# A two-layer decoder step: the last expert pair added by a one-hot product, the first pair's tokens picked by one-hot products, a separate place for the mixing weights

## The chip, the core and the metric

One core of one Trainium2 chip runs the whole step. The metric is device time in microseconds (us) of one execution, the median of several runs; lower is better.

## What is computed

Two layers over 288 tokens (256 of a prompt, 32 of eight decoding sequences), model width 1024, all in float32. Layer 0 mixes tokens by latent attention, layer 1 by a spatial gating unit. After the mixer each layer adds a mixture of experts and then a gated projection ("ple"):

```
pg = softmax(t @ w_rg + b_rg)              # 4 groups, top 1
pe = softmax(le of that group)             # 8 experts, top 2
w  = pg_top * pe_top / sum(pe_top)
y  = sum over the 2 experts of w * (silu(t @ w_gate) * (t @ w_up)) @ w_down
h  = h + y
h  = h + sigmoid(rmsnorm(h) @ w_ple_gate) * (p @ w_ple_proj)
```

with 32 experts of hidden width 256. So a token belongs to exactly two experts, both of one group, and they may or may not be in the same pair of experts.

## The kernel before, in words

**Weights.** All weights lie in HBM as a stream of 250 slots of 1 MB. SyncE loads them in order into a ring of 12 slots (`load_slot`, `load_rounds`); a load waits for the semaphore `slot_free`, which TensorE raises as it uses up slots. The slots of one layer's experts are six per pair: four with gate and up weights, two with down weights. Before them stands one slot with the projection of `ple`, behind them four with its gate. The third gate slot and all behind it wait for `y12_in2`, the landing of the last `y12` load.

**Routing** (`moe(L)` on each engine). TensorE forms the router's sums. VectorE (L848 to L887) finds group and experts, computes the rank of each token in its expert, and from that a row number `row`: two experts form a pair, each with a window of 64 rows, 128 rows in all. ScalarE takes one exponential (L563) for the routing weights, in the middle of copying the eight tiles of the projection `prj` out of PSUM (L565; TensorE makes them in `project`, L1325). `members(n)` (L895, L899) builds for pair n the one-hot table `member` (six blocks of 128x128: first and second expert choice, by three token tiles) and steps `row` on. `list_pair` (L1334) multiplies it with token numbers and weights, and `take_list` (L903, L904) stores the token number and destination row of the 128 rows in `slots`, and the weights in `gr`.

**Pairs.** For each of the 16 pairs GpSimd gathers the tokens' rows from HBM (`gather`, L335) into `x_sel`, two buffers. TensorE transposes them (`x_turn`, L1360), ScalarE and VectorE copy the halves into `xT` (L569, L917), TensorE runs gate and up (L1374), ScalarE and VectorE form the activation (L573, L922), TensorE transposes it (L1367), ScalarE copies (L577), TensorE runs down (L1383), and the result, scaled by the routing weight, goes into `y_sb` (L581 ScalarE, L927 VectorE). GpSimd scatters it to `y_rows` in HBM (`scatter`, L344): 2 x 288 rows, one for each token and choice. If an expert has more than 64 tokens, a loop on all engines (`If(most > WIN)`) does the rest in further passes; with these inputs it is skipped.

**Combination and gate.** When the scatter of the last pair has landed, GpSimd loads `y_rows` into `y12` with six transfers (L400). VectorE adds the two choices (L976), TensorE transposes 128-column tiles of the sum (`combine`, L1457), VectorE adds them to `h` (L688) and multiplies by the gain (L692). TensorE then runs the first tile of the gate (`gate_part`, L1446), mixed with the transposes and with eight products that sum the squares for the norm (`square_part`, L1462; ScalarE squares, L609). ScalarE takes the root (L457), VectorE the reciprocal (L708); then follow seven more tiles of eight products. In layer 0 ScalarE, after the root, starts three loads: the spatial mixing weights `ws` and `wss` and their bias `bs` (L613). Their place in memory overlaps `y12`. VectorE masks them (L984, L985), and TensorE sums their columns (L1486, L1488) behind the third gate tile.

**End.** After the last norm VectorE scales the even tiles of the output, GpSimd the odd ones (L422); ScalarE issues all eight stores, even ones first (L643, L646).

The lines that say most of this are:

```
pool.wait_ge(sem(f"y_put{L}_{b}"), 16 * (PAIRS // 2))       # before the y12 loads, both b
pe.wait_ge(sem(f"x_got{L}_0"), 16)                           # before the first x_turn
pe.wait_ge(sem("comb"), 3 * L + 3)                           # before the first combine
pe.wait_ge(sem("ws_m"), 2)                                   # before L1486
```

## Time and profile before

| | |
|---|---|
| median of 3 runs | 1240.37 us (1238.86 to 1242.16) |
| the profiled execution | 1241.1 us, span of its instructions 1239.3 us |
| TensorE busy | 1081.3 us, 87% of the span |
| VectorE, ScalarE, GpSimd busy | 363.0, 193.5, 112.8 us |
| transfers | 306.80 MB, mean 248 GB/s |
| mean granted TensorE clock | 0.94 of 2.4 GHz |

How the views are read. A line of the *timeline* has the start, the busy time, the engine (PE TensorE's products, PEld its weight loads, DVE VectorE, ACT ScalarE, POOL GpSimd, SP SyncE; with a q, its queue issuing a transfer), the line of the kernel, the operation, output<-inputs and their shapes, how many instructions are merged, and in brackets the idle time before and what ended it. TensorE needs two passes for a float32 product, so the profile shows two instructions for each, while a transpose is one. A line of a table of *windows* has the window, its length, the busy time (and instructions) of PE, PEld, DVE, ACT and POOL, then the granted clock (1.00 is 2.4 GHz, 0.50 is 1.2 GHz), the busy share of the 16 transfer engines, and GB/s. The *chain of waits* follows the work that ended last back to the start and gives shares of the span.

### The profile page before, as it was taken

The numbers are of one execution on the slowest core, as the hardware profiler recorded it, in microseconds if no ns is written. First come the engines' busy times: TensorE is split into PE (matmuls) and PEld (weight loads), VectorE is DVE, ScalarE is ACT, GpSimd is POOL, SyncE is SP. The second block draws the span as 40 slices with busy tenths as digits, with TensorE's granted clock in tenths as the row PEclk, the third lists the DMA queues.
The fourth block names the chain that finished last, engine by engine and source line by source line (L and its number), as shares of the span: only waits on it lengthen the run. The fifth ranks groups of instructions, "written<-read, shape, count | busy, mean of one in ns | idle before, by whom it ended". The sixth has DMA issues, their size and how long they took to land.

```text
span 1239.3 us, 14327 instructions
## 1 busy us (share of the span) xinstructions
PE 1081.3 (87%) x5212; PEld 664.5 (54%) x5212; DVE 363.0 (29%) x897; ACT 193.5 (16%) x396; POOL 112.8 (9%) x150
## 2 busy tenths in 40 slices
PE   5898879899988986579999999999989998887393
PEld 4675546644433332467777777777654443332172
DVE  1243332522222210335223644421242221211254
ACT  2121211311111111112111211000111111111121
POOL 0134100111111100100000000000011111110101
PEclk9998889999999999679999999999989999999787
DMA  9628636289999996843333323333359999999401
GB/s 384 247 76 246 194 111 270 77 339 420 418 419 418 420 420 278 326 178 121 136 132 110 133 102 111 120 132 108 128 195 391 417 417 419 419 420 415 158 38 38
DMA packets 62596, 306.80 MB, mean 248 GB/s; under 512 B 13730, under 2 KB 23170, under 8 KB 30402
## 3 DMA queue, kind: packets, MB, share of 16 engines
q1 hardware_dynamic: 45360, 275.93, 56.1%
q0 software_dynamic: 13632, 22.58, 5.6%
q10 hardware_dynamic: 3538, 7.39, 1.6%
q8 instruction: 44, 0.72, 0.2%
q14 instruction: 22, 0.18, 0.0%
HBM read 308.88 MB, written 21.08 MB: 266 GB/s over the span
## 4 chain that ended last, share of the span: by engine, by line
PE 63%; DMA 25%; DVE 5%; issue 4%; ACT 1%; POOL 0%; SPq 0%; POOLq 0%; ACTq 0%; DVEq 0%
DMA ring_sb<-stream 22%; PE ps L1511 15%; PE ps L1374 10%; PE ps L1559 8%; PE ps L1383 4%; PE ps L1446 3%; PE ps L1293 3%; PE ps L1108 2%; PE ps L1128 2%; PE ps L1334 2%; DMA scr_sb<-y_rows 1%; DMA scr_sb<-bs 1%; PE ps L1325 1%; PE ps L1462 1%; PE ps L1457 1%
## 5 line engine op out<-in xcount | busy, mean ns | idle before, releaser
L1374 PE MATMUL ps<-ring_sb,scr_sb 128*64 128x512 f32 x1024 | 236.9, 609 | 40.5 <-DMA ring_sb<-stream 40.4
L1511 PE MATMUL ps<-hn_sb,ring_sb 128*128 128x288 f32 x768 | 194.9, 408 | 0.0
L1374 PEld LDWEIGHTS ps<-ring_sb,scr_sb 128*64 128x64 f32 x1024 | 79.0, 140 | 193.5 <-issue 193.5
L1511 PEld LDWEIGHTS ps<-hn_sb,ring_sb 128*128 128x128 f32 x768 | 142.6, 190 | 37.3 <-DVE hn_sb L692 0.3
L1383 PE MATMUL ps<-ring_sb,scr_sb 128*64 128x512 f32 x512 | 120.3, 613 | 2.8 <-ACT scr_sb L577 2.8
L1559 PE MATMUL ps<-scr_sb,ring_sb 128*128 128x288 f32 x384 | 95.3, 407 | 0.0
L922 DVE SCALAR_TENSOR_TENSOR scr_sb<-ps,scr_sb 128x256 f32<-128x256 f32 x32 | 15.5, 484 | 266.8 <-ACT scr_sb L573 266.8
L1559 PEld LDWEIGHTS ps<-scr_sb,ring_sb 128*128 128x128 f32 x384 | 72.2, 190 | 19.4
L1446 PE MATMUL ps<-scr_sb,ring_sb 128*128 128x288 f32 x256 | 70.0, 427 | 0.0
L1383 PEld LDWEIGHTS ps<-ring_sb,scr_sb 128*64 128x64 f32 x512 | 34.7, 139 | 62.2 <-issue 57.5
L335 POOL DMA_INDIRECT scr_sb<-hn_rows,scr_sb x32 | 32.4, 1014 | 297.6 <-DVE scr_sb L904 273.8
L1446 PEld LDWEIGHTS ps<-scr_sb,ring_sb 128*128 128x128 f32 x256 | 51.0, 201 | 14.7
L1011 DVE TENSOR_TENSOR scr_sb<-ps,rstd_sb 128x288 f32<-128x288 f32 x48 | 21.8, 453 | 124.4 <-PE ps L1511 124.4
L573 ACT ACTIVATE scr_sb<-ps,scr_sb 128x256 f32<-128x256 f32 x32 | 15.2, 474 | 239.7 <-PE ps L1374 239.7
L927 DVE TENSOR_SCALAR scr_sb<-ps,scr_sb 128x512 f32<-128x512 f32 x32 | 24.0, 751 | 92.8 <-PE ps L1383 92.8
L1334 PE MATMUL ps<-tv_sb,scr_sb 128*128 128x4 f32 x384 | 45.5, 248 | 2.4 <-DVE scr_sb L895 2.4
L1334 PEld LDWEIGHTS ps<-tv_sb,scr_sb 128*128 128x128 f32 x384 | 45.8, 193 | 3.4 <-DVE scr_sb L895 2.5
L344 POOL DMA_INDIRECT y_rows<-scr_sb x32 | 31.7, 992 | 173.9 <-DVE scr_sb L927 170.4
L325 POOL MEMSET scr_sb<- 128x2048 f32 x2 | 3.6, 1802 | 465.6 <-DVE h_sb L688 465.6
L414 POOL DMA_DIRECT2D ring_sb<-row_pages x64 | 34.5, 540 | 115.4 <-issue 100.3
L581 ACT ACTIVATE scr_sb<-ps,scr_sb 128x512 f32<-128x512 f32 x32 | 22.0, 687 | 143.2 <-PE ps L1383 143.2
L1360 PEld LDWEIGHTS ps<-const_sb,scr_sb 128*128 128x128 f32 x256 | 28.0, 143 | 27.1 <-issue 24.5
(245 smaller groups left out, 1077.1 us busy)
## 6 DMA issues: line engine op xcount, KB each, us to landing
ring_sb<-stream SPq DMA_DIRECT2D x250, 1024.0 KB, 19.7
scr_sb<-key_pages SPq DMA_DIRECT2D x64, 192.0 KB, 3.4
ring_sb<-row_pages POOLq DMA_DIRECT2D x64, 128.0 KB, 3.2
scr_sb<-y_rows POOLq DMA_DIRECT2D x8, 512.0 KB, 5.1
hn_rows<-scr_sb ACTq DMA_DIRECT2D x4, 512.0 KB, 3.2
h_sb<-x SPq DMA_DIRECT2D x1, 1152.0 KB, 5.5
y_out<-hn_sb ACTq DMA_DIRECT2D x8, 144.0 KB, 1.8
scr_sb<-bs ACTq DMA_DIRECT2D x1, 640.0 KB, 13.2
```

The lines of the kernel that those rows point to most:

```text
L335: pool.indirect_dma_start(out=x_sel[:, c % 2, :], out_offset=None, in_=hn_rows[L], in_offset=bass.IndirectOffsetOnAxis(ap=slots[:, c, 0:1] ...
L344: pool.indirect_dma_start(out=y_rows[L], out_offset=bass.IndirectOffsetOnAxis(ap=slots[:, c, 1:2], axis=0), in_=y_sb[:, c % 2, :], in_offs ...
L414: pool.dma_start(ring(c % 7, (2 * b + pg) * KV, KV), io["row_pages"][bass.ds(page, 1)].rearrange("a p n -> (a p) n")).then_inc(sem(f"rows_ ...
L1108: last = mm(ps[0:mn, m, 0:T], ring(S_IN, at, mn), hn_t[:, k, :], start=(k == 0), stop=(k == KD - 1))
L1293: last = mm(bank(m % 4, T), ring(S_O, m * D + k * P, P), oT[:, k, :], start=(k == 0), stop=(k == H - 1))
L1334: last = mm(ps[:, 7, 0:4], member[:, q, :], tv[:, q // 3, q % 3, :], start=(q == 0), stop=(q == 5))
L1360: last = nc.tensor.transpose(ps[:, k // 4, (k % 4) * P:(k % 4) * P + P], x_sel[:, b, k * P:(k + 1) * P], ident)
L1374: last = mm(ps[64 * a:64 * a + 64, 2 + b, :], xT[:, k, 64 * a:64 * a + 64], slot(a + 2 * (k // 4))[:, (k % 4) * 512:(k % 4) * 512 + 512], ...
L1383: last = mm(ps[64 * a:64 * a + 64, 5 + n, :], aT[:, k, 64 * a:64 * a + 64], slot(4 + k)[:, a * D + n * 512:a * D + n * 512 + 512], start=( ...
L1446: last = mm(bank(PLE_BANK[m % 4], T), ring(s, (m % 2) * D + k * P, P), hgp[:, k, :], start=(k == 0), stop=(k == KD - 1))
L1511: last = mm(bank((i + 1) % 4, T), ring(s, (i % 2) * D + k * P, P), hn_t[:, k, :], start=(k == 0), stop=(k == KD - 1))
L1559: last = mm(bank((m + 1) % 4, T), ring(s, (at % 16) * P, P), uT[:, k, :], start=(k == 0), stop=(k == FT - 1))
```

## The change

- **Last pair.** Its result is no longer scattered and loaded again. GpSimd scatters zeros (`y_none`) into its rows instead, right after the last gather, and the `y12` loads wait for the scatters of pairs 0 to 14 and for that one. VectorE's adds of the two choices are gone: `combine` takes both halves of `y12` as products with the identity, and a product of `y_sb` with `oh_last`, the transposed one-hot table of the last pair, is added in the same PSUM sum. `oh_last` is made at pair 13: `both` adds the halves of `member` into `m01`, TensorE transposes it, ScalarE copies.
- **First pair.** It isn't gathered. `m01` of pair 0 is multiplied with the token rows `hn_tok` that are in memory: 8 tiles x 3 token tiles = 24 products, straight into the banks that `x_turn` filled. The list of pair 0 now comes after them, the lists of pairs 1 and 2 between gate/up products of pair 0.
- **Projection.** It uses four PSUM banks instead of two, and six of its tiles stand ahead of the rank products, the rest right behind. The exponential stands behind five copies instead of two.
- **Norm of the gate.** The squares are summed on VectorE (`sum_sq`), and one product (`sum_norm`) stands behind the second gate tile, in place of the eight between the products of the first.
- **Mixing weights.** `ws`, `wss`, `bs` have a place beyond `y12`; their loads start after the last pair instead of after the root.
- **End.** SyncE issues the stores of the odd tiles.

```diff
+    m01 = M.take(3 * P).rearrange("p (t r) -> p t r", t=3)
+    oh_last = M.take(T)
...
+    U.at = max(U.at, SCR - 5 * SLOT + 6 * D)
+    wsT = U.take(G * 2 * P).rearrange("p (g r) -> p g r", g=8)
...
@@ SyncE, at the end
+        for k in range(1, KD, 2):
+            sp.wait_ge(sem("y_p"), k // 2 + 1)
+            sp.dma_start(io["y_out"][:, k, :], hn_t[:, k, :]).then_inc(sem("out"), 16)
...
@@ GpSimd
+            pool.memset(y_none, 0.0).then_inc(sem("x_clear"), 1)
...
-            for c in range(3):
+            for c in range(1, 3):
                 gather(c)
-            for n in range(PAIRS):
+            for n in range(PAIRS - 1):
                 if n + 3 < PAIRS:
                     gather(n + 3)
+                    if n + 3 == PAIRS - 1:
+                        scatter_none()
                 scatter(n)
...
-                pool.wait_ge(sem(f"y_put{L}_{b}"), 16 * (PAIRS // 2))
+                pool.wait_ge(sem(f"y_put{L}_{b}"), 16 * (PAIRS // 2 - b))
+            pool.wait_ge(sem("y_none"), 16 * (L + 1))
...
@@ ScalarE
-                if m == 2:
+                if m == 5:
                     act.wait_ge(sem("sel"), 2 * L + 2)
                     nc.scalar.activation(ex, dx, ACT.Exp).then_inc(sem("ex"), 1)
...
@@ VectorE
+            def both(n):
+                dve.wait_ge(sem(f"member{L}"), 2 * n + 1)
+                nc.vector.tensor_tensor(m01, member[:, 0:3, :], member[:, 3:6, :], ALU.add).then_inc(sem("m01"), 1)
             members(0)
+            both(0)
             take_list(slots[:, 0, :], gr[:, 0, :], 1)
             members(1)
+            copy_x(1)
...
-            for t, (t0, tn) in enumerate(TOK):
-                dve.wait_ge(sem(f"y12_in{t}"), 32 * L + 32)
-                nc.vector.tensor_tensor(y12[0:tn, 0, t, :], y12[0:tn, 0, t, :], y12[0:tn, 1, t, :], ALU.add).then_inc(sem("comb"), 1)
...
+                if k >= 1:
+                    sum_sq(ple, k - 1)
...
@@ TensorE
+            pe.wait_ge(sem("m01"), 2 * L + 1)
+            for k in range(KD):
+                for t, (t0, tn) in enumerate(TOK):
+                    last = mm(ps[:, k // 4, (k % 4) * P:(k % 4) * P + P], hn_tok[0:tn, t, k * P:(k + 1) * P], m01[0:tn, t, :],
+                              start=(t == 0), stop=(t == 2))
+            last.then_inc(sem(f"x_ps{L}"), 1)
...
-            pe.wait_ge(sem("comb"), 3 * L + 3)
+            pe.wait_ge(sem("cnt"), L + 1)
+            for t in range(3):
+                pe.wait_ge(sem(f"y12_in{t}"), 32 * L + 32)
+            pe.wait_ge(sem("oh"), L + 1)
+            pe.wait_ge(sem(f"y_sb{L}"), 2 * PAIRS)
...
-                    last = nc.tensor.transpose(ps[:, k % 4, t0:t0 + tn], y12[0:tn, 0, t, k * P:(k + 1) * P], ident[0:tn, 0:tn])
+                    for a in range(2):
+                        mm(ps[:, k % 4, t0:t0 + tn], y12[0:tn, a, t, k * P:(k + 1) * P], ident[0:tn, 0:tn],
+                           start=(t == 0 and a == 0), stop=False)
+                mm(bank(k % 4, T), y_sb[:, 1, k * P:(k + 1) * P], oh_last, start=False, stop=True).then_inc(sem("h_part"), 1)
```

Where instructions move, at three places. In each row: the line, the operation, output<-inputs, the shape, the semaphores waited for, and how many. TensorE from the second projection tile on to the first pair, before (L1325 projection, L134x ranks, L1334 lists, L1360 `x_turn`, L1374 gate/up):

```order
L1325 MATMUL ps<-scr_sb,ring_sb 128x288 x3
L1325 MATMUL ps<-scr_sb,ring_sb 128x288 [waits prj]
L1343 MATMUL ps<-scr_sb,const_sb 128x32
L1334 MATMUL ps<-tv_sb,scr_sb 128x4 [waits member0,tv]
L1334 MATMUL ps<-tv_sb,scr_sb 128x4 [waits slots0,member0]
L1360 MATMUL ps<-const_sb,scr_sb 128x128 [waits x_got0_0,cnt,prj]
L1374 MATMUL ps<-ring_sb,scr_sb 64x512 [waits slot_full2,slot_full1,xT0]
L1374 MATMUL ps<-ring_sb,scr_sb 64x512 x7
```

and in the change (L1356 projection, L1385 token products, L1365 lists, L1409 gate/up):

```order
L1356 MATMUL ps<-scr_sb,ring_sb 128x288 [waits hr_a]
L1374 MATMUL ps<-scr_sb,const_sb 128x32
L1385 MATMUL ps<-scr_sb 128x128 [waits m01]
L1385 MATMUL ps<-scr_sb 128x128 x23
L1365 MATMUL ps<-tv_sb,scr_sb 128x4 [waits member0,tv]
L1409 MATMUL ps<-ring_sb,scr_sb 64x512 [waits slot_full1,slot_full2,xT0,prj]
L1409 MATMUL ps<-ring_sb,scr_sb 64x512 x3
L1365 MATMUL ps<-tv_sb,scr_sb 128x4 [waits slots0,member0]
L1409 MATMUL ps<-ring_sb,scr_sb 64x512 x4
```

The 24 products stand where transposes of gathered rows stood, and two lists have moved in among the gate/up products. ScalarE at the exponential of the routing weights, before:

```order
L559 DMA hn_rows<-scr_sb 128x1024 [waits hr_a]
L565 ACTIVATE scr_sb<-ps 128x288 [waits prj_ps] x2
L563 ACT_TABLE_LOAD
L563 ACTIVATE scr_sb<-scr_sb 128x15 [waits sel]
L565 ACTIVATE scr_sb<-ps 128x288 [waits prj_ps] x6
```

and in the change:

```order
L582 DMA hn_rows<-scr_sb 128x1024 [waits hr_a]
L588 ACTIVATE scr_sb<-ps 128x288 [waits prj_ps] x5
L586 ACT_TABLE_LOAD
L586 ACTIVATE scr_sb<-scr_sb 128x15 [waits sel]
L588 ACTIVATE scr_sb<-ps 128x288 [waits prj_ps] x3
```

Three more copies, each of which waits for a projected tile, stand ahead of the table load. TensorE at the first tiles of the combination, before:

```order
L1457 MATMUL ps<-const_sb,scr_sb 128x128 [waits comb]
L1457 MATMUL ps<-const_sb,scr_sb 128x128
L1457 MATMUL ps<-const_sb,scr_sb 128x32
L1457 MATMUL ps<-const_sb,scr_sb 128x128 x2
L1457 MATMUL ps<-const_sb,scr_sb 128x32
```

and in the change:

```order
L1504 MATMUL ps<-const_sb,scr_sb 128x128 [waits y12_in2,oh,y12_in1,y_sb0,y12_in0,cnt]
L1504 MATMUL ps<-const_sb,scr_sb 128x128 x3
L1504 MATMUL ps<-const_sb,scr_sb 128x32 x2
L1506 MATMUL ps<-scr_sb 128x288
L1504 MATMUL ps<-const_sb,scr_sb 128x128 x4
```

A tile was three transposes; it is now seven products, and the first waits for the loads themselves.

## Rows read from the trace of the kernel before

**Rows 1.** The page's chain that ended last, shares of the span by line:

```profile
DMA ring_sb<-stream 22%; PE ps L1511 15%; PE ps L1374 10%; PE ps L1559 8%; PE ps L1383 4%; PE ps L1446 3%; PE ps L1293 3%; PE ps L1108 2%; PE ps L1128 2%; PE ps L1334 2%; DMA scr_sb<-y_rows 1%; DMA scr_sb<-bs 1%; PE ps L1325 1%; PE ps L1462 1%; PE ps L1457 1%
```

**Rows 2.** Table of windows, pairs of layer 0, early and late:

```profile
258.00:270.00 12.00, 10.48 (x52) 4.89 (x54) 3.10 (x7) 3.32 (x5) 1.84 (x2) 0.86 0.96 389
...
450.00:480.00 30.00, 23.80 (x113) 9.12 (x115) 3.67 (x6) 4.29 (x8) 1.93 (x2) 1.00 0.99 412
```

**Rows 3.** Timeline, layer 0, from the projection to the first pair:

```profile
230.58 2.21 PE L1325 MATMUL ps<-scr_sb,ring_sb 128*128 128x288 f32 x8
...
234.51 1.28 ACT L563 ACT_TABLE_LOAD   x1
...
236.75 0.22 ACT L563 ACTIVATE scr_sb<-scr_sb 128x15 f32<-128x15 f32 x1 [0.96 <-DVE scr_sb L870]
...
239.37 0.96 DVE L895 TENSOR_TENSOR scr_sb<-const_sb,scr_sb 128x768 f32<-128x768 f32 x1
...
244.49 3.60 PE L1325 MATMUL ps<-scr_sb,ring_sb 128*128 128x288 f32 x8
...
250.86 7.09 PE L1374 MATMUL ps<-ring_sb,scr_sb 128*64 128x512 f32 x32
```

**Rows 4.** Timeline, layer 1, first membership table and first pair:

```profile
902.60 0.96 DVE L895 TENSOR_TENSOR scr_sb<-const_sb,scr_sb 128x768 f32<-128x768 f32 x1
...
915.69 6.66 PE L1374 MATMUL ps<-ring_sb,scr_sb 128*64 128x512 f32 x30
```

**Rows 5.** Timeline, prices of TensorE passes at full clock:

```profile
260.76 1.40 PE L1334 MATMUL ps<-tv_sb,scr_sb 128*128 128x4 f32 x12
...
717.12 0.61 PE L1534 MATMUL ps<-scr_sb 128*128 128x128 f32 x4
717.65 0.40 PE L1535 MATMUL ps<-scr_sb 32*128 32x32 f32 x2
717.99 4.15 PE L1511 MATMUL ps<-hn_sb,ring_sb 128*128 128x288 f32 x16
```

**Rows 6.** Layer 0, last two pairs to the combination; second line: that scatter's landing:

```profile
478.02 0.96 POOL L344 DMA_INDIRECT y_rows<-scr_sb  x1 [14.56 <-DVE scr_sb L927]
...
DMA to landing us min/median/max: 7.6/7.6/7.6
...
491.92 0.75 DVE L927 TENSOR_SCALAR scr_sb<-ps,scr_sb 128x512 f32<-128x512 f32 x1 [4.80 <-PE ps L1383]
...
497.07 3.18 POOL L400 DMA_DIRECT2D scr_sb<-y_rows  x6 [2.58 <-DMA y_rows<-scr_sb]
...
505.96 2.35 DVE L976 TENSOR_TENSOR scr_sb<-scr_sb 128x1024 f32<-128x1024 f32 x2 [2.31 <-DMA scr_sb<-y_rows]
...
508.37 3.51 PE L1457 MATMUL ps<-const_sb,scr_sb 128*128 128x128 f32 x12 [16.56 <-DVE scr_sb L976]
```

**Rows 7.** Timeline, layer 1, the first transposes of the combination:

```profile
1174.83 3.51 PE L1457 MATMUL ps<-const_sb,scr_sb 128*128 128x128 f32 x12 [16.39 <-DVE scr_sb L976]
```

**Rows 8.** Timeline, layer 0, gate tiles and row sums of the mixing weights:

```profile
524.96 7.92 PE L1446 MATMUL ps<-scr_sb,ring_sb 128*128 128x288 f32 x32
...
540.88 3.78 PE L1486 MATMUL ps<-scr_sb,const_sb 128*128 128x128 f32 x16 [7.99 <-DVE scr_sb L985]
...
548.13 21.72 PE L1446 MATMUL ps<-scr_sb,ring_sb 128*128 128x288 f32 x80
```

**Rows 9.** Table of windows, layer 0, the clock around the combination:

```profile
492.00:497.00 5.00, 0.00 (x0) 0.00 (x0) 0.67 (x1) 2.08 (x3) 0.96 (x1) 0.73 0.11 39
...
516.00:520.00 4.00, 4.00 (x15) 2.63 (x14) 1.65 (x4) 0.66 (x2) 0.00 (x0) 0.73 1.01 426
```

**Rows 10.** Timeline, last norm, last scaling and last stores:

```profile
1222.22 1.30 PE L1496 MATMUL ps<-scr_sb,const_sb 128*128 128x288 f32 x2 [3.90 <-DVE scr_sb L701]
...
1226.20 3.94 POOL L422 TENSOR_TENSOR hn_sb<-hn_sb,rstd_sb 128x288 f32<-128x288 f32 x4 [59.02 <-DVE rstd_sb L708]
...
1229.91 1.96 ACTq L646 DMA_DIRECT2D y_out<-hn_sb  x4
```

114 lines of the change are left out of this document (63 added, 51 removed).

## The prediction

> **What bounds the kernel now.** I read the chain of waits first: the loads of the weight stream (`ring_sb<-stream`) lead with 22%, before the products of the spatial gating (L1511) and of the pairs (L1374) [rows 1]. The stream's share lies in two blocks, the two runs of sixteen expert pairs. The table of windows says how such a block behaves: the transfer engines are 0.96 busy from the first pair on and 0.99 near its end [rows 2]. So inside a block a weight slot is paid at the transfer rate, the block ends when the last slots have landed, and a delay of TensorE counts only where it frees the first slots later; the whole block then shifts. Around each block the stretches bounded by engines are read from the timeline: routing to first pair [rows 3, 4], last pair to the first product of the gate [rows 6, 7], and the gate of layer 0 [rows 8]. The rest (attention, spatial gating) the change doesn't touch.
>
> **1. Routing to the first pair.** Before, the first gate/up product starts 11.5 us after the first membership table (L895, 239.37 to 250.86) in layer 0 and 13.1 us after it in layer 1 (902.60 to 915.69) [rows 3, 4].
>
> The exponential of the routing weights now stands behind five copies of the projection, and its table load moves with it. The fifth copy can end at about 236.45 (TensorE starts at 230.58 and needs 1.0 to 1.1 for a tile [rows 3], the fifth is there by 236.05; a copy is about 0.4); then 1.28 us of table load, so it starts near 237.75, not at 236.75 [rows 3]. Everything up to the membership table hangs on it: +1.0 us in layer 0; layer 1 has a somewhat later routing against the same copies, so I take +0.65. The Trainium skill (ScalarE: Activation LUTs, What ACT_TABLE_LOAD costs) adds a drain of about 1.38 us to the load; by it the term would be +2.4. The trace doesn't bear this out: the load ends at 235.79 and the exponential runs 0.96 us later, less than that drain [rows 3].
>
> From the membership table on: 0.96 for it, 0.2 for the step of `row`, 0.55 for the sum of the two halves (128x384, an estimate between the 0.45 of 288 columns and the 0.7 of 512 columns in the same engine's timeline) and 0.05 of signal: TensorE starts 1.75 after. Then 24 products, 48 passes. A 128-column pass costs 0.133 at full clock (717.12 to 717.65, four of them), one on 32 rows 0.17 at most (717.65 to 717.99, two) [rows 5]: 32 and 16 of them, with the latter taken at 0.15, give 6.6 us. VectorE copies its half of the tokens only behind the first list and the second membership table: list 1.3 [rows 5], taking it 0.3, table and row step 1.1, copy 0.7, signals 0.1. Sum 11.8 us. Net: layer 0 +1.0+11.8-11.5 = **+1.3**, layer 1 +0.65+11.8-13.1 = **-0.65**. That projection and gather no longer stand ahead (3.60 us at a low clock, from 244.49 [rows 3]) is in these differences. Two lists of about 1.25 us now lie between gate/up products of pair 0; slots are freed by those products, so the block's transfers start 2.5 us later in each layer: **+5.0**. The clearing of `y_none` on GpSimd, the zero scatter against the missing last one, and the one-hot transposes at pair 13 lie beside a block bounded by transfers: nothing; without that cover the transposes would be three passes of 0.14. Region 1 together: **+5.7**.
>
> **2. Last pair to the combination.** Before: last scatter, then the six loads of `y12` from 497.07, the last adds at 505.96, the first transpose at 508.37 [rows 6]. Now the loads wait only for the scatter of pair 14, issued at 478.02 and landed 7.6 later [rows 6], at 485.6. With 0.55 to issue, the 8.9 that they took (497.07 to 505.96), and 1.0 because the last stream slots still move, they are in at 496.1 on the old clock of time. The last pair's `y_sb` is ready at 492.7 (491.92 + 0.75) [rows 6], so the loads decide. 508.4 - 496.1 = **-12.3**; layer 1 has the same pattern, with an idle time of 16.39 before its first transpose where layer 0 has 16.56 [rows 6, 7]; I take **-12.1**.
>
> **3. Combination.** Three transposes become six products and one of 288 columns. At full clock per tile: 8 x 0.133 + 4 x 0.17 + 2 x 0.25 = 2.2 us, the 0.25 from sixteen passes in 3.98 [rows 5]; eight tiles 17.9, with the gate's first sixteen passes 4.0: 21.9 us. Before, it took 16.6 (508.37 to 524.96, the square sums on TensorE included) [rows 6, 8]. **+5.3 and +5.7.** VectorE's share per tile (add, gain, now also the sum of squares, some 1.4 us) stays below 2.2. The clock: before, TensorE is done when the last copy of `y_sb` begins (491.9), and the granted clock has fallen within 492 to 497, mean 0.73 [rows 9]. In layer 0 the new start at 496 lies behind that fall, so some 5 to 6 us of work run at half speed: **+2.5**; in layer 1 I take none. Bounds: 0 and, with both layers low for about 10 us, +9.
>
> **4. Gate.** `sum_norm` behind the second tile adds 0.5 in each layer; the reciprocal behind it is late by 4 us against seven tiles of 3.9 of which VectorE needs about 3.0 each, so it has caught up at the last tile. In layer 0 TensorE starts 32 passes (two tiles, 7.9 us) at 524.96 and then idles to 540.88, of which rows 8 name 7.99 as the wait for the masked weights (`bs` and its fellows, loaded too late); the row-sum products take 7.25 at half clock, to 548.13 [rows 8]. Now these loads start at about 494 and have landed by 508 even if they need 13 us as before. From the second tile: 3.9, then sum, root and reciprocal 3.93 as at the end (TensorE from 1222.22, scaling from 1226.20, less 0.05 [rows 10]) and masks 1.6 (1280 columns, an estimate from the 0.96 of 768 columns [rows 3]) on VectorE, with the third tile beside them, products 32 passes at 0.15 = 4.85: 14.4 against 23.2: **-8.8** with its own `sum_norm`. Layer 1: **+0.5**.
>
> **5. End.** SyncE issues the odd tiles as GpSimd finishes them; its last ends at 1230.14, while before ScalarE issued them from 1229.91 to 1231.87 [rows 10]: **-1.2**.
>
> **Sum.** Layer 0: +3.8 - 12.3 + 5.3 + 2.5 - 8.8 = -9.5. Layer 1: +1.9 - 12.1 + 5.7 + 0.5 = -4.0. End -1.2. Together -14.7 on the profiled execution's 1241.1, which is 0.7 over the median of the runs: 1226.4 for it, **1225.7** for the median.
>
> **Rivals.**
> *A, all goes a little better*: the clock doesn't fall in layer 0, and the `y12` loads meet an almost empty queue. Less 2.5 and less 2: **1221**. For it: the stream's rate has already sunk after 480; against: the fall of the clock in rows 9.
> *B, contention*: the `y12` loads take transfer time from the last pair's slots, which the last products wait for. Most of the load's 8.9 us would have to lie in the busy queue; with 3 to 5 us in each layer about +8: **1234**. Against: the block's transfers have thinned out by the time the scatter has landed (485.6) and the down slots are needed at 488. The Trainium skill (DMA: Bandwidth & Descriptors, Queues, rings and completion order) says that each transfer engine takes turns between its queues packet by packet; by that rule the shares are about equal, and B is what follows if loads and last slots really overlap. No row shows such an overlap yet.
> *C, the token products run at half clock*: TensorE idles for about 1.8 us ahead of them, and before the clock fell at this place (the eight passes from 244.49 took 3.60 where 2.0 is full speed [rows 3]). 48 passes at the 0.236 of the row-sum products (sixteen in 3.78 [rows 8]) cost 4.7 more, lists and copies a little: +5 in a layer, **1231** for one, **1236** for both. Against: two more tiles of dense 288-column passes (2.2 us) now stand right ahead of the gap.
> *D, slower*: the clock stays at 1.2 GHz through the whole combination and the gate's first tile in both layers, as it did for ten of the 16.6 us before. Per tile 12 x 0.236 + 2 x 0.48 = 3.8, eight 30.1, gate 7.8: 37.9 for 21.9, +16 twice less the 2.5 already in: **1255**. It decides once the low stretch of both layers together exceeds some 40 us (each us at half clock costs about 0.42). Against: before, the clock was back within 516 to 520, some 10 us after a sparser start [rows 9].
> *E, it doesn't do what it says*: something else still holds the `y12` loads till the last pair (the zero scatter landing late, say). Then +24 and -3 for the adds: **1247**.
>
> **Chances.** Forecast 0.47, A 0.20, B 0.12, C 0.15, D 0.03, E 0.03. About 0.3% (3.7 us) is what a measurement of this kernel can tell from no change; faster means below 1236.6. D and E are slower; of C's upper end, 0.03 falls within. Faster 0.91, same 0.03, slower 0.06. The range takes A with its spread, the forecast, B, and C up to both layers: 1216 to 1236; what is left out is D, E and the edges.
>
> **What would show it.** First gate/up product 11 to 12 us after the first membership table, with the 48 passes in 6 to 7 us; the exponential about 1 us later against the routing; the first `y12` load 8 us after the scatter of pair 14 and ahead of the last pair's end; the first combining product about 4 us after the last `y_sb` copy in layer 0; combination and first gate tile in 22 to 25 us; no wait on `bs`. Wrong would be: products of the last pair that wait for the stream beyond 485, a combination near 38 us, or a first pair that starts more than 3 us later than before.

## The result, and the profile after

| | before | after |
|---|---|---|
| median of the runs, us | 1240.7 (1238.9 to 1243.8, 6 runs) | 1254.0 (1248.5 to 1259.2, 6 runs) |
| ratio, with its 95% interval | | 1.0117 [1.0096, 1.0138] |
| profiled execution, span, us | 1239.3 | 1252.6 |
| mean granted clock of that execution | | 0.948 |
| first membership table to first gate/up product, layer 0 / 1 | 11.5 / 13.1 | 19.6 / 13.6 |
| the 32 gate/up passes of pair 0, first start to last end, with what stands among them | 7.1 / 7.1 | 15.8 / 14.6 |
| first gate/up to the last pair's second down step | 239.1 / 240.9 | 247.2 / 250.3 |
| from there to the first combining product | 18.4 / 18.3 | 12.2 / 9.0 |
| from that to the first gate product behind the last combining product | 12.7 / 12.3 | 27.7 / 21.8 |
| from that to the gate's end | 48.8 / 31.2 | 34.2 / 29.8 |
| first combining product to the gate's second tile | 16.6 / 16.2 | 29.6 / 23.7 |
| gate's second tile to the gate's end | 44.9 / 27.3 | 32.3 / 27.8 |

The change made the kernel slower by 1.2%, where 1.2% faster was forecast. The rows of the table are differences of start times in the timelines (layer 0 / layer 1), the same instruction in each kernel; the later tables use them too. The "second down step" is the last pair's second weight slot, which stands 1.8 us behind its first down product. The "first gate product behind the last combining product" is the fifth of the eight products of the gate's first tile. From there to the second tile it is 3.9 us where TensorE still sums the squares (before, e2, e7, e11, e12) and 1.9 us in the other kernels. The prediction's region 3 ran to the second tile (16.6 us before, 508.37 to 524.96); that cut has its own row.

The chain of waits by line, of the kernel after (its line numbers: 1409 gate/up, 1418 down, 1385 token products, 1504 and 1506 combination, 1488 gate, 1365 lists, 1555 and 1603 spatial gating):

```profile
PE 67%; DMA 21%; DVE 5%; issue 4%; ACT 2%; POOL 1%; SPq 0%; POOLq 0%; ACTq 0%; DVEq 0%
DMA ring_sb<-stream 17%; PE ps L1555 15%; PE ps L1409 11%; PE ps L1603 8%; PE ps L1418 4%; PE ps L1488 3%; PE ps L1504 3%; PE ps L1322 2%; PE ps L1137 2%; PE ps L1365 2%; PE ps L1157 2%; DMA scr_sb<-y_rows 2%; PE ps L1385 2%; DMA y_rows<-scr_sb 1%; PE ps L1506 1%
```

Against [rows 1] the token products (L1385, 2%) are new on the chain, the combination has gone from 1% to 4% (L1504 and L1506), and the stream of weights has lost five points of its share. That is no gain: the kernel is slower, and more of its time lies outside the stream. Where that time lies is plainest in the windows of layer 0 around the first pair. First the kernel before, then the kernel after (columns: window, its length, busy time and count on TensorE, its weight loads, VectorE, ScalarE, GpSimd; granted clock; busy share of the transfer engines; GB/s):

```profile
242.00:246.00 4.00, 2.87 (x17) 2.48 (x18) 2.54 (x9) 0.00 (x0) 1.33 (x2) 0.89 0.09 24
246.00:250.00 4.00, 3.50 (x18) 2.39 (x17) 0.48 (x3) 1.10 (x3) 0.76 (x1) 0.68 0.40 91
250.00:254.00 4.00, 4.00 (x25) 1.98 (x26) 3.10 (x14) 0.32 (x1) 0.98 (x1) 1.00 0.95 397
254.00:258.00 4.00, 4.00 (x21) 1.19 (x18) 0.00 (x0) 0.00 (x0) 0.00 (x0) 1.00 0.59 212
258.00:262.00 4.00, 2.48 (x22) 2.24 (x22) 1.08 (x2) 2.63 (x4) 0.00 (x0) 1.00 1.01 422
```

```profile
234.00:238.00 4.00, 3.15 (x17) 2.44 (x17) 0.76 (x3) 0.12 (x1) 0.00 (x0) 0.90 0.73 262
238.00:242.00 4.00, 4.00 (x14) 3.10 (x14) 0.00 (x0) 0.00 (x0) 0.00 (x0) 0.50 0.00 0
242.00:246.00 4.00, 4.00 (x14) 3.04 (x13) 0.00 (x0) 0.00 (x0) 0.00 (x0) 0.50 0.00 0
246.00:250.00 4.00, 4.00 (x18) 3.39 (x16) 0.00 (x0) 0.60 (x1) 0.00 (x0) 0.50 0.00 0
250.00:254.00 4.00, 1.97 (x8) 1.27 (x10) 1.86 (x5) 0.00 (x0) 0.00 (x0) 0.50 0.00 0
254.00:258.00 4.00, 4.00 (x14) 1.87 (x10) 0.00 (x0) 0.00 (x0) 0.00 (x0) 0.50 0.48 158
258.00:262.00 4.00, 4.00 (x14) 2.05 (x15) 1.51 (x6) 0.00 (x0) 1.07 (x1) 0.50 0.26 109
262.00:266.00 4.00, 4.00 (x20) 1.84 (x18) 0.05 (x1) 0.00 (x0) 0.00 (x0) 0.69 0.38 76
266.00:270.00 4.00, 3.66 (x20) 1.47 (x18) 2.62 (x13) 1.27 (x1) 1.01 (x1) 1.00 0.90 373
```

Read the last three columns: granted clock, busy share of the transfer engines, GB/s. Before, the granted clock dips for some 4 us and the transfer engines are near full use from 250 on. After, it is 0.50 (1.2 GHz) from 238 to past 262, although TensorE shows busy in all of it but the 2 us between 250.8 and 252.8, and the transfers stand still until the products of pair 0 start at 252.8 and free slots; they are back in full use at 266. From the membership table to the first full use it is 11 us before (with one more dip at 254 to 258) and 33 us after. From there on the block is the stream's [rows 2], and the shift stays.

The token products themselves, by form, in layer 1, where their clock was 1.00 (lines by engine and form, 908 to 922 us; busy us, mean ns of one, idle before):

```profile
L1385 PE MATMUL ps<-scr_sb 128*128 128x128 f32 x32 | 5.7, 300 | 1.2 <-DVE scr_sb L934 1.2
L1385 PE MATMUL ps<-scr_sb 32*128 32x128 f32 x16 | 3.9, 321 | 0.0
L1409 PE MATMUL ps<-ring_sb,scr_sb 128*64 128x512 f32 x4 | 2.0, 1080 | 2.0 <-issue 2.0
```

and the same in layer 0 at the low clock (234 to 256 us):

```profile
L1385 PE MATMUL ps<-scr_sb 128*128 128x128 f32 x32 | 8.6, 416 | 1.2 <-DVE scr_sb L934 1.2
L1385 PE MATMUL ps<-scr_sb 32*128 32x128 f32 x16 | 5.7, 453 | 0.0
```

Together the 48 passes take 8.5 us in layer 1 and 13.3 in layer 0; forecast were 6.6. The timeline of layer 0 shows the weight loads going by fours and twos, with a break at each change:

```profile
234.85 13.26 PE L1385 MATMUL ps<-scr_sb 128*128 128x128 f32 x48 [1.18 <-DVE scr_sb L934]
237.95 0.50 PEld L1385 LDWEIGHTS ps<-scr_sb 32*128 32x128 f32 x2 [0.22 <-issue]
238.67 0.93 PEld L1385 LDWEIGHTS ps<-scr_sb 128*128 128x128 f32 x4 [0.23 <-issue]
239.82 0.50 PEld L1385 LDWEIGHTS ps<-scr_sb 32*128 32x128 f32 x2 [0.22 <-issue]
...
250.94 0.95 DVE L916 TENSOR_TENSOR scr_sb<-const_sb,scr_sb 128x768 f32<-128x768 f32 x1
251.93 0.17 DVE L920 TENSOR_SCALAR scr_sb<-scr_sb 128x6 f32<-128x6 f32 x1
252.01 0.68 DVE L929 COPY scr_sb<-ps 128x512 f32<-128x512 f32 x1
252.79 1.98 PE L1409 MATMUL ps<-ring_sb,scr_sb 128*64 128x512 f32 x4 [2.03 <-issue]
```

The last four rows are what stands ahead of the first gate/up product: second membership table, row step, VectorE's copy, in the order that the prediction had, and TensorE idle for 2.03 us.

The products of pair 0 that follow take 15.8 us, with two lists among them, where they took 7.09 [rows 3]. Pair 1's gate/up products then start at 276.3, 23.5 us after pair 0's; before it was 16.4 us. The timeline of TensorE alone, first pair 1 of the kernel before, then pair 0 (lists L1365, gate/up L1409) and the start of pair 1 of the kernel after:

```profile
267.27 7.04 PE L1374 MATMUL ps<-ring_sb,scr_sb 128*64 128x512 f32 x32
```

```profile
256.40 2.73 PE L1365 MATMUL ps<-tv_sb,scr_sb 128*128 128x4 f32 x12
...
264.38 1.53 PE L1365 MATMUL ps<-tv_sb,scr_sb 128*128 128x4 f32 x12
265.84 2.79 PE L1409 MATMUL ps<-ring_sb,scr_sb 128*64 128x512 f32 x12
...
276.27 7.04 PE L1409 MATMUL ps<-ring_sb,scr_sb 128*64 128x512 f32 x32
```

At the other end of the block, in layer 0:

```profile
496.49 3.17 POOL L423 DMA_DIRECT2D scr_sb<-y_rows  x6 [7.45 <-DMA y_rows<-scr_sb]
...
498.21 3.65 PE L1418 MATMUL ps<-ring_sb,scr_sb 128*64 128x512 f32 x16 [0.47 <-ACT scr_sb L600]
...
503.00 0.35 ACTq L634 DMA_DIRECT2D scr_sb<-ws  x1
...
512.19 3.03 PE L1504 MATMUL ps<-const_sb,scr_sb 128*128 128x128 f32 x12 [10.33 <-DMA scr_sb<-y_rows]
```

The first `y12` load now goes out ahead of the last pair's down products, as forecast, but the loads are all in only at 511.8, 15.3 us after the first went out. Before, the last landed at 506.9, 9.8 us after the first; the 8.9 of the prediction end at the start of the last two additions [rows 6], of which the second waited for that landing. Then the combination, by windows:

```profile
508.00:512.00 4.00, 0.00 (x0) 0.00 (x0) 0.00 (x0) 0.00 (x0) 0.00 (x0) 0.50 0.40 156
512.00:516.00 4.00, 3.81 (x14) 3.41 (x15) 0.00 (x0) 0.00 (x0) 0.00 (x0) 0.50 0.79 265
516.00:522.00 6.00, 6.00 (x24) 5.13 (x22) 1.87 (x5) 0.89 (x2) 0.00 (x0) 0.50 1.01 423
522.00:528.00 6.00, 6.00 (x21) 5.14 (x21) 1.19 (x3) 0.44 (x1) 0.00 (x0) 0.50 1.01 429
528.00:534.00 6.00, 6.00 (x31) 5.05 (x29) 2.38 (x6) 0.89 (x2) 0.00 (x0) 0.77 1.01 423
```

The clock that fell in the idle time stays at 1.2 GHz for 18 us of work here; before it was back some 10 us after the first transpose [rows 9].

Of the gate, [rows 8] had a wait of 7.99 us for the masked weights; the group that answers to it (lines by engine, 538 to 575 us) has 0.3:

```profile
L1528 PE MATMUL ps<-scr_sb,const_sb 128*128 128x128 f32 x16 | 2.1, 281 | 0.3 <-DVE scr_sb L1015 0.3
```

One difference is not the change's. In the two profiled executions attention ended 6.8 us apart (the last routing product of layer 0 starts at 228.3 before, 221.5 after), in code that is the same. In the profiled executions of the experiments below that point lies between 221.3 and 228.7, with both values met by kernels of either kind (221.3 and 228.3 by two that share the changed kernel's attention word for word). So it is the spread of one execution, and times between marks are compared, not positions in the span.

### The profile page after: what moved, and what is told of

It is laid out like the page before. It is cut to its first block, busy times and chain, and to the rows that moved or that the text cites. A ratio compares the mean times of both kernels' runs of the same rounds, so it can differ in the third digit from the quotient of the medians.

```text
span 1252.6 us, 14833 instructions
## 1 busy us (share of the span) xinstructions
PE 1118.7 (89%) x5446; PEld 698.9 (56%) x5446; DVE 362.8 (29%) x911; ACT 193.9 (15%) x398; POOL 113.0 (9%) x150
## 4 chain that ended last, share of the span: by engine, by line
PE 67%; DMA 21%; DVE 5%; issue 4%; ACT 2%; POOL 1%; SPq 0%; POOLq 0%; ACTq 0%; DVEq 0%
DMA ring_sb<-stream 17%; PE ps L1555 15%; PE ps L1409 11%; PE ps L1603 8%; PE ps L1418 4%; PE ps L1488 3%; PE ps L1504 3%; PE ps L1322 2%; PE ps L1137 2%; PE ps L1365 2%; PE ps L1157 2%; DMA scr_sb<-y_rows 2%; PE ps L1385 2%; DMA y_rows<-scr_sb 1%; PE ps L1506 1%
## 5 line engine op out<-in xcount | busy, mean ns | idle before, releaser
L1409 PE MATMUL ps<-ring_sb,scr_sb 128*64 128x512 f32 x1024 | 246.7, 629 | 44.8 <-DMA ring_sb<-stream 40.8
L1409 PEld LDWEIGHTS ps<-ring_sb,scr_sb 128*64 128x64 f32 x1024 | 80.8, 143 | 200.2 <-issue 200.1
L1418 PE MATMUL ps<-ring_sb,scr_sb 128*64 128x512 f32 x512 | 120.3, 613 | 2.1 <-ACT scr_sb L600 1.9
L1603 PE MATMUL ps<-scr_sb,ring_sb 128*128 128x288 f32 x384 | 95.3, 407 | 0.0
L950 DVE SCALAR_TENSOR_TENSOR scr_sb<-ps,scr_sb 128x256 f32<-128x256 f32 x32 | 15.5, 484 | 259.6 <-ACT scr_sb L596 259.6
L1488 PE MATMUL ps<-scr_sb,ring_sb 128*128 128x288 f32 x256 | 64.8, 409 | 0.0
L1040 DVE TENSOR_TENSOR scr_sb<-ps,rstd_sb 128x288 f32<-128x288 f32 x48 | 21.8, 453 | 124.4 <-PE ps L1555 124.4
L1488 PEld LDWEIGHTS ps<-scr_sb,ring_sb 128*128 128x128 f32 x256 | 48.9, 191 | 13.6
L1365 PEld LDWEIGHTS ps<-tv_sb,scr_sb 128*128 128x128 f32 x384 | 49.1, 205 | 6.0 <-issue 5.9
L709 DVE TENSOR_TENSOR h_sb<-h_sb,ps 128x288 f32<-128x288 f32 x32 | 14.5, 452 | 130.8 <-PE ps L1603 54.0
L475 ACT ACTIVATE scr_sb<-h_sb 128x288 f32<-128x288 f32 x48 | 21.0, 438 | 193.9 <-DVE h_sb L709 193.9
L1504 PE MATMUL ps<-const_sb,scr_sb 128*128 128x128 f32 (+1 forms) x192 | 34.1, 332 | 16.9 <-DMA scr_sb<-y_rows 16.9
L1365 PE MATMUL ps<-tv_sb,scr_sb 128*128 128x4 f32 x384 | 49.1, 257 | 0.0
L1504 PEld LDWEIGHTS ps<-const_sb,scr_sb 128*128 128x128 f32 (+1 forms) x192 | 33.1, 244 | 23.5 <-issue 19.9
## 6 DMA issues: line engine op xcount, KB each, us to landing
ring_sb<-stream SPq DMA_DIRECT2D x250, 1024.0 KB, 19.2
```

The lines of the kernel that those rows point to most:

```text
L1365: last = mm(ps[:, 7, 0:4], member[:, q, :], tv[:, q // 3, q % 3, :], start=(q == 0), stop=(q == 5))
L1409: last = mm(ps[64 * a:64 * a + 64, 2 + b, :], xT[:, k, 64 * a:64 * a + 64], slot(a + 2 * (k // 4))[:, (k % 4) * 512:(k % 4) * 512 + 512], ...
L1418: last = mm(ps[64 * a:64 * a + 64, 5 + n, :], aT[:, k, 64 * a:64 * a + 64], slot(4 + k)[:, a * D + n * 512:a * D + n * 512 + 512], start=( ...
L1488: last = mm(bank(PLE_BANK[m % 4], T), ring(s, (m % 2) * D + k * P, P), hgp[:, k, :], start=(k == 0), stop=(k == KD - 1))
L1504: mm(ps[:, k % 4, t0:t0 + tn], y12[0:tn, a, t, k * P:(k + 1) * P], ident[0:tn, 0:tn], start=(t == 0 and a == 0), stop=False)
L1603: last = mm(bank((m + 1) % 4, T), ring(s, (at % 16) * P, P), uT[:, k, :], start=(k == 0), stop=(k == FT - 1))
```

## The experiments

Every kernel was timed beside runs of the kernel before on the same chip; the ratio is to those. Their medians went from 1236.3 to 1240.7, so ratios are the measure, and for round numbers below 0.1% is 1.24 us.

| kernel | median us | ratio [interval] | table to gate/up | gate/up to last down | down to combination | combination |
|---|---|---|---|---|---|---|
| after (profile above) | 1254.0 | 1.0117 [1.0096, 1.0138] | 19.6 / 13.6 | 247.2 / 250.3 | 12.2 / 9.0 | 27.7 / 21.8 |
| e1_first_by_gather | 1230.5 | 0.9916 [0.9889, 0.9944] | 13.1 / 13.1 | 239.7 / 243.0 | 11.5 / 10.2 | 22.0 / 22.1 |
| e2_first_alone | 1260.0 | 1.0156 [1.0132, 1.0180] | 19.7 / 19.5 | 246.3 / 247.4 | 19.2 / 19.2 | 12.3 / 11.9 |
| e3_ws_late | 1262.5 | 1.0176 [1.0130, 1.0222] | 13.7 / 13.8 | 243.9 / 245.8 | 9.9 / 9.8 | 27.7 / 27.6 |
| e4_four_before | 1249.7 | 1.0102 [1.0064, 1.0139] | 16.0 / 16.0 | 244.2 / 247.6 | 12.1 / 9.3 | 21.8 / 21.8 |
| e5_lists_ahead | 1256.6 | 1.0137 [1.0105, 1.0168] | 19.8 / 19.8 | 244.1 / 247.6 | 12.0 / 9.7 | 22.2 / 27.9 |
| e6_adds | 1219.6 | 0.9842 [0.9815, 0.9870] | 13.1 / 11.4 | 239.1 / 242.6 | 14.1 / 11.4 | 18.8 / 19.9 |
| e7_last_alone | 1235.8 | 0.9995 [0.9965, 1.0024] | 13.2 / 11.4 | 239.0 / 243.0 | 11.0 / 8.9 | 24.0 / 23.7 |
| e8_fill | 1231.0 | 0.9934 [0.9909, 0.9960] | 11.5 / 13.1 | 239.8 / 242.8 | 13.8 / 13.5 | 19.0 / 19.0 |
| e9_adds_fill | 1217.3 | 0.9812 [0.9782, 0.9843] | 11.5 / 13.3 | 238.5 / 242.3 | 15.0 / 11.9 | 15.3 / 13.6 |
| e10_dense_around | 1248.0 | 1.0080 [1.0048, 1.0112] | 15.7 / 18.9 | 243.9 / 246.2 | 8.9 / 9.8 | 27.7 / 23.9 |
| e11_ws_alone | 1230.2 | 0.9941 [0.9922, 0.9960] | 13.1 / 11.4 | 239.5 / 240.3 | 22.1 / 18.5 | 13.6 / 12.2 |
| e12_last_adds | 1227.1 | 0.9911 [0.9884, 0.9938] | 11.4 / 11.8 | 239.9 / 242.9 | 10.8 / 11.7 | 21.7 / 19.5 |
| e13_late_start | 1248.0 | 1.0076 [1.0053, 1.0098] | 20.1 / 20.1 | 239.7 / 244.2 | 12.2 / 9.4 | 28.0 / 21.8 |
| e14_two_tiles | 1235.5 | 0.9990 [0.9972, 1.0008] | 8.8 / 8.8 | 243.2 / 245.5 | 12.0 / 10.1 | 21.8 / 25.7 |
| e15_tiles_sorted | 1244.2 | 1.0038 [1.0016, 1.0060] | 11.0 / 11.0 | 244.1 / 250.0 | 12.2 / 8.8 | 21.9 / 21.8 |
| e16_combine_sorted | 1212.7 | 0.9780 [0.9749, 0.9810] | 13.1 / 11.4 | 240.2 / 242.2 | 12.4 / 11.9 | 12.8 / 12.7 |
| e17_all | 1222.8 | 0.9895 [0.9853, 0.9936] | 9.6 / 9.6 | 246.0 / 245.9 | 12.5 / 17.7 | 12.7 / 12.7 |
| e18_tokens_sorted | 1226.9 | 0.9915 [0.9882, 0.9948] | 11.0 / 10.9 | 244.5 / 247.3 | 12.4 / 18.5 | 12.8 / 12.8 |

The last four columns are of each kernel's profiled execution, layer 0 / layer 1, "combination" from its first product to the first gate product behind its last one.

### Which part costs: e1, e2

e1_first_by_gather puts the first pair back, with the order of projection, lists and exponential that went with it, and keeps the rest. Its main part:

```diff
-            for c in range(1, 3):
+            for c in range(3):
                 gather(c)
...
-            pe.wait_ge(sem("m01"), 2 * L + 1)
-            for k in range(KD):
-                for t, (t0, tn) in enumerate(TOK):
-                    last = mm(ps[:, k // 4, (k % 4) * P:(k % 4) * P + P], hn_tok[0:tn, t, k * P:(k + 1) * P], m01[0:tn, t, :],
...
+            pe.wait_ge(sem(f"x_got{L}_0"), 16)
+            x_turn(0)
+            list_pair(3, 2)
```

> The changed kernel with the first pair's tokens by gather and transposes again, and the order of projection, lists and exponential as before; the last pair's one-hot product, the weights' own home and the rest stay. Theory 1 (the first pair's token products and what the clock does around them cost about 22 us of the 25 us by which the forecast was missed): 1230 to 1234 us, first gate/up to last pair's down start 237 to 239 us in both layers, gate/up of pair 0 back to 7 us. Rival (the loss lies in the combination and the end, and the first pair's change is worth less than 5 us): 1249 us or more.

e2_first_alone is the reverse: the kernel before with the first pair's change alone, the projection's order included. So neither run tells the order of the projection from the token products.

> The kernel before with the first pair's change alone: token products, the two lists among pair 0's gate/up products, the projection's order. Theory 1: 1258 to 1264 us (before plus 18 to 24). Rival 2 (the clock and the lists cost little by themselves, and the loss needs the other parts): 1240 to 1246 us.

Measured: 1230.5 (-0.84%) and 1260.0 us (+1.56%). Theory 1 holds in both. The first pair's change costs 19.5 us by itself, and without it the rest is worth 10.4 us. In the marks: table to gate/up and gate/up to last down are back within 2.1 us of the values before in e1 (layer 1's 243.0 us, against 240.9, miss the 237 to 239 that were expected, as in most kernels with the last pair's product), and go to 19.6 and 247 in e2.

### The clock ahead of the first pair: e4, e10

```diff
+            for j in range(4):
+                mm(bank(0), ident, hn_tok[:, 0, 0:512], start=True, stop=True)
             pe.wait_ge(sem("m01"), 2 * L + 1)
```

> The changed kernel with four idle 512-column products put in front of the wait for the membership sum, so that TensorE has no gap between the projection and the token products. Theory 4 (the granted clock falls at 237 us because of the gap at 234 us): the clock stays at 1.00 through the token products in layer 0, 48 passes take 7 to 9 us and not 13.3, pair 0's gate/up 8 to 10 us and not 15.8, total 8 to 14 us less. Rival (the clock falls whatever stands in the gap, since 128-column passes do not hold it): clock 0.50 from about 237 to 264 us again, total 0 to 6 us more for the four products in both layers.

e10_dense_around has three of them there, and three into another bank behind list 1:

> The changed kernel with three idle 512-column products ahead of the token products and three behind list 1, where TensorE waits 2.0 us for VectorE's way to the tokens' copy. Theory 4 (idle stretches bring the clock down, and the low clock is half of the first pair's loss): clock 1.00 through token products, lists and pair 0's gate/up in both layers, membership table to first gate/up 15 to 16.5 us, pair 0's gate/up 6.6 us, first gate/up to last down 241 to 244 us, total 4 to 10 us below the changed kernel (1244 to 1250 us). Rival (128-column and 4-column passes bring it down by themselves): low clock in one or both layers as before, total 1254 to 1260 us.

Measured: 1249.7 and 1248.0 us. In e4 the clock stood at 1.00 through the token products in both layers and fell for 3.4 us behind them; in e10 it held through them in layer 0 and fell for 6.8 us in layer 1. Both ratios lie a little below the changed kernel's 1.0117, with intervals that overlap its; the 8 to 14 us expected of e4 did not come. So a dense stretch ahead does not hold the clock reliably here. And e3_ws_late (below), whose first pair is the changed kernel's own, had 1.00 through the token products of both layers with nothing put in. What follows is a limit rather than a cause: with the clock held, table to gate/up is 13.7 us and not 19.6, but first gate/up to last down is still 244 to 246 and not 239 to 241, and even e10 stays 0.8% above the kernel before. Ahead of the first gate/up product Theory 4 explains some 6 us in a layer where the clock falls. The rest of the clock's price lies behind it: pair 0's gate/up passes with their two lists take 10.3 us where the clock is 1.00 throughout (layer 0 of e10 and of e14), 11.6 and 12.3 us in e3, and 15.8 and 14.6 us in the changed kernel, where it was 1.2 GHz for most of them.

### The lists: e5

```diff
+            pe.wait_ge(sem("tv"), 2 * (L + 1))
+            list_pair(1, None)
             pe.wait_ge(sem("m01"), 2 * L + 1)
...
-            list_pair(1, None)
+            list_pair(2, 1)
...
-                    if n == 0 and k == 1:
-                        list_pair(2, 1)
-                    if n == 0 and k == 4:
-                        list_pair(3, 2)
                 last.then_inc(sem(f"h_ps{L}"), 1)
+                if n == 0:
+                    list_pair(3, 2)
```

> The changed kernel with another order of the lists alone: list 1 ahead of the token products, list 2 between them and pair 0's gate/up products, list 3 behind these. Theory 5a (the token products cost their own 48 passes; the two lists among pair 0's gate/up add about 3 us a layer, and list 1's way over VectorE can lie beside the passes): pair 0's gate/up back from 6.6 to 15.8 us to 3.7 to 7.3, membership table to first gate/up 12 to 14 us where the clock holds, total 3 to 8 us less than the changed kernel (1242 to 1250 us; the interval would still hold the kernel before's time only at its end). Rival 5b (the clock's fall costs all of it and falls anyway): within 2 us of the changed kernel, 1248 to 1256 us.

Measured: 1256.6 us, within the changed kernel's interval: rival 5b. The clock was low in both layers through token products and pair 0 (19.8 us each; pair 0's gate/up passes, now with no list among them, took 8.7 us), so what the other order would give at the full clock did not show.

### A microsecond late at pair 0: e13

The kernel of e1 with eight idle products behind list 3.

> The kernel of e1_first_by_gather with eight idle 512-column products (7.0 us at the full clock) between list 3 and pair 0's gate/up products, in both layers. Theory 6 (the transfers of the weights stand still with a full ring until pair 0's gate/up frees slots, and are the bound from then to the last pair, so a microsecond of delay there costs a microsecond at the end): 12 to 14 us more than e1_first_by_gather, 1242 to 1246 us, and the time from first gate/up to the last down unchanged. Rival (the ring's stock takes it up): less than 5 us more, 1230 to 1235 us, and the time from first gate/up to last down shorter by the delay.

Measured: 1248.0 us (1242 to 1246 were expected), 1.60% above e1, some 19 to 20 us, and 7.0 more in each layer's table to gate/up, with gate/up to last down nearly unchanged (239.7 / 244.2 against 239.7 / 243.0). The delay of 14 us is passed on whole; of the rest, 6.0 us lie in layer 0's combination, which this time ran at the low clock for 19 us (28.0 against 22.0). Theory 6 holds: at this place a microsecond costs a microsecond, and the ring takes up nothing.

### What the token products cost: e14, e15

e14_two_tiles runs the products of two of the three token tiles (`TOK[0:2]`, `stop=(t == 1)`).

> The changed kernel with the token products of two of the three token tiles: the first pair gets no rows of tokens 256 to 287, which is left out of the computation. 32 passes and not 48. Theory 1 (passes are paid in full where they stand): 0.18 us a pass at the full clock, 0.28 at the low one, so 2.8 to 4.5 us a layer, 1245 to 1249 us. Rival (the clock's fall and the way over VectorE set the time, the passes hide in it): 1251 us or more.

Measured: 1235.5 us, 18.5 us below the changed kernel, where 5 to 9 were expected. The 32 passes took 3.8 us, 0.12 each (230 to 262 us, by form):

```profile
L1385 PE MATMUL ps<-scr_sb 128*128 128x128 f32 x32 | 3.8, 278 | 1.2 <-DVE scr_sb L934 1.2
```

So sixteen further passes had made 8.5 us out of 3.8. Either passes on 32 rows are slow, or what is slow is going back and forth. e15_tiles_sorted leaves nothing out and changes the order alone:

```diff
-            for k in range(KD):
-                for t, (t0, tn) in enumerate(TOK):
-                    last = mm(ps[:, k // 4, (k % 4) * P:(k % 4) * P + P], hn_tok[0:tn, t, k * P:(k + 1) * P], m01[0:tn, t, :],
-                              start=(t == 0), stop=(t == 2))
+            for k, t in [(k, t) for k in range(KD) for t in range(2)] + [(k, 2) for k in range(KD)]:
+                tn = TOK[t][1]
+                last = mm(ps[:, k // 4, (k % 4) * P:(k % 4) * P + P], hn_tok[0:tn, t, k * P:(k + 1) * P], m01[0:tn, t, :],
+                          start=(k % 4 == 0 and t == 0), stop=(k % 4 == 3 and t == 2))
```

> The changed kernel with the same 48 token passes in another order: first the 32 passes on 128 rows for all eight blocks, then the 16 on 32 rows. Nothing is left out. Theory 7 (a change between 128 and 32 rows holds back the next weight load, some 0.2 us a change, 16 changes before and 1 now; in the changed kernel's layer 1 the starts stand 0.11 us apart among equal passes and 0.20 to 0.21 around a change): the 48 passes take 5.4 to 5.9 us at the full clock and not 8.5, total 6 us less by that alone (1248) and up to 16 less if the clock then holds as in e14_two_tiles (1238). Rival 8 (the 32-row passes themselves are slow, 0.29 us each): 8.5 us for the 48 passes and 1252 to 1256 us.

By form, 225 to 265 us:

```profile
L1385 PE MATMUL ps<-scr_sb 128*128 128x128 f32 x32 | 3.8, 278 | 1.2 <-DVE scr_sb L934 1.2
...
L1385 PE MATMUL ps<-scr_sb 32*128 32x128 f32 x16 | 2.0, 276 | 0.0
```

5.8 us for all 48, 0.12 each whatever the rows, and 1244.2 us in all, 9.8 below the changed kernel. The weight loads tell the same:

```profile
237.49 5.62 PEld L1385 LDWEIGHTS ps<-scr_sb 128*128 128x128 f32 x48 [1.65 <-DVE scr_sb L934]
```

48 loads in a row without a break, where the changed kernel's go by fours and twos. Theory 7 is borne out, rival 8 is not: with one change of rows in place of fifteen the passes take 2.7 us less at the full clock, 0.19 us a change. The total fell by more than 2 x 2.7, and a part of the rest may be the clock: in none of the eight layers of e14, e15, e17 and e18 was the clock low for more than 2 us between table and gate/up (behind it, in layer 1 of e15, it was low for 12), while it was low for 6 us or more in six of the twelve layers of kernels that go back and forth (after, e2, e3, e4, e5, e10). That is a count over a few executions, not a proof that the changes bring the clock down.

### The last pair and the combination: e7, e11, e12, e6, e8, e9, e16

e7_last_alone is the kernel before with the last pair's one-hot product alone, e11_ws_alone with the mixing weights' home and early loads alone.

> The kernel before with the last pair's one-hot product alone (no home for the mixing weights, the norm's sums on TensorE as before, stores as before). Theory 1 with additivity (first pair plus 19.5, all the rest minus 10): the weights' home gave 9 us in layer 0's gate, so the last pair and its combination are worth 1 us or less: 1236 to 1242 us. Rival (the last pair is worth the forecast's 12 minus 5 us in each layer): 1226 to 1232 us.

> The kernel before with the mixing weights' home and their early loads alone. Theory (gate of layer 0 waits 8 us for them in the kernel before, and nothing else comes of it): the gate of layer 0 from 48.8 to 36 to 41 us, the y_rows loads of layer 0 up to 3 us longer, total 1229 to 1234 us. Rival (the early loads push the y_rows loads back by what they save): 1236 us or more.

Measured: 1235.8 us (no difference that can be told) and 1230.2 us (-0.59%, 7.3 us). The home of the weights gives what was forecast of it. The last pair's product gives nothing: in e7 the combination begins 7.4 and 9.4 us sooner and lasts 11.3 and 11.4 us longer than before. In layer 0 the gate, from its second tile on, is 13.0 us shorter (31.9 against 44.9), although the weights' loads still start behind the root: `bs` lands 5.7 us after its issue and not 13.2, with the transfer engines less full by then. Before, the window from 528 to 532 had a busy share of 1.01 and 411 GB/s; e7 has

```profile
528.00:532.00 4.00, 4.00 (x18) 3.16 (x17) 0.00 (x0) 1.68 (x2) 0.00 (x0) 1.00 0.70 246
```

So in the marks the wait and the combination together lose 6 us, and what makes up for it is the gate's wait, the same wait that the weights' home removes in e11 (13.7 us there).

e12_last_adds and e6_adds put VectorE's three additions back, in e7 and e1:

```diff
+            for t, (t0, tn) in enumerate(TOK):
+                dve.wait_ge(sem(f"y12_in{t}"), 32 * L + 32)
+                nc.vector.tensor_tensor(y12[0:tn, 0, t, :], y12[0:tn, 0, t, :], y12[0:tn, 1, t, :], ALU.add).then_inc(sem("comb"), 1)
...
-                    for a in range(2):
-                        mm(ps[:, k % 4, t0:t0 + tn], y12[0:tn, a, t, k * P:(k + 1) * P], ident[0:tn, 0:tn],
-                           start=(t == 0 and a == 0), stop=False)
+                    mm(ps[:, k % 4, t0:t0 + tn], y12[0:tn, 0, t, k * P:(k + 1) * P], ident[0:tn, 0:tn],
+                       start=(t == 0), stop=False)
```

> The kernel of e7_last_alone (the last pair's one-hot product alone) with VectorE's three additions back, four passes for a block and not seven. Theory (the seven passes ate the last pair's gain): total 1222 to 1230 us, 6 to 13 us below e7_last_alone. Rival (the three additions give back on VectorE what TensorE saves, and what e6_adds won came from chance): 1233 to 1238 us.

> The kernel of e1_first_by_gather with VectorE's three additions of the two row sets back, so that the combination has four passes for a 128-column block and not seven. Theory 2 (the combination is bound by TensorE's passes): combination and first gate tile from 22.0 us to 16 to 18, last pair's down to first combining product 1 to 2.5 us longer by the additions, total 4 to 9 us less than 1230.5 us (1222 to 1227). Rival (VectorE's sums and gains bound it, or the additions come out of the transfers' shadow): 1229 to 1235 us.

Measured: 1227.1 and 1219.6 us, 0.84% below e7 and 0.75% below e1. With three products fewer in each block the last pair's change is worth 11 us, layer 0's shorter gate (12.9 us in e12's marks) included. (e6's profiled execution shows less of it than its median, its clock was lower in the combination than e1's.)

e8_fill puts twelve idle 512-column products into the wait for `y12` of e1, e9_adds_fill ten into that of e6.

```diff
+            for j in range(12):
+                mm(bank(0), ident, y_sb[:, 0, 0:512], start=True, stop=True)
```

> The kernel of e1_first_by_gather with twelve idle 512-column products (0.60 us each at the full clock, 7.2 us) behind the last pair's down products, where TensorE waits 8 to 10 us for the y_rows loads. Theory 4 (the low clock of the combination is owed to this idle time): the granted clock is 1.00 from the combination's first product on, combination and first gate tile 16 to 19 us and not 22 to 27.7, total 4 to 12 us less than 1230.5 us. Rival (the combination's own 128-column passes bring the clock down, whatever TensorE did before): as e1_first_by_gather within 2 us.

> The kernel of e6_adds with ten idle 512-column products (0.88 us each in e8_fill) behind the last pair's down products. Theory (clock and passes both price the combination, and VectorE comes next): the clock stays at 1.00 from there on, combination and first gate tile from 18.8 and 19.9 us to 14 to 16, total 3 to 8 us less than e6_adds (1211 to 1217 us). Rival (VectorE's norm sums and gains bound the combination by now, or the ten products reach past the landing): 1218 to 1223 us.

In e8 they held the clock in both layers. First e1, then e8, windows of layer 1 from the wait on:

```profile
1147.00:1152.00 5.00, 0.05 (x1) 0.08 (x1) 0.00 (x0) 0.00 (x0) 0.00 (x0) 0.63 0.12 42
1152.00:1158.00 6.00, 6.00 (x23) 5.20 (x23) 0.82 (x2) 0.45 (x1) 0.00 (x0) 0.50 0.91 336
1158.00:1164.00 6.00, 6.00 (x36) 5.27 (x37) 2.38 (x7) 0.89 (x2) 0.00 (x0) 0.96 0.04 16
```

```profile
1154.00:1160.00 6.00, 6.00 (x16) 2.65 (x15) 0.00 (x0) 0.00 (x0) 0.00 (x0) 1.00 0.40 147
1160.00:1166.00 6.00, 6.00 (x42) 5.11 (x40) 1.87 (x5) 0.88 (x2) 0.00 (x0) 1.00 0.52 213
```

23 passes in six microseconds in e1 at 1.2 GHz, 42 in e8 at 2.4 GHz; the combination went from 22.0 to 19.0 us. But the total stayed at e1's (ratios 0.9934 and 0.9916): twelve products took 10.6 us, not the 7.2 that I had reckoned (each is two passes here), and reached 2 to 4 us past the landing. In e9, with ten of them, the ratio is 0.9812 against e6's 0.9842, with intervals that overlap: no difference that can be told. The combination was 15.3 and 13.6 us. What the clock costs the combination is thus 3 us a layer where its low stretch is 6 us, and 8.7 where it is 18 (27.7 against 19.0).

e16_combine_sorted takes e9 and sorts the first four blocks by rows, as e15 did:

```diff
+            for t in range(3):
+                for k in range(4):
+                    turn(k, t)
+            for k in range(4):
+                last_in(k)
```

> The kernel of e9_adds_fill with the first four blocks of the combination sorted in the same way: all 128-row products, the 32-row ones, the last pair's products (2 changes of rows and not 8). Theory 7: 6 changes at 0.2 us, 1.2 us a layer, total 1214 to 1217 us. Rival (VectorE starts later, since the first block is ready later, and is the bound): 1217 to 1220 us.

Measured: **1212.7 us, ratio 0.9780 [0.9749, 0.9810]**, the best of all: 2.2% faster than the kernel before. The combination takes 12.8 us, as before, with the last pair's product in it. Against e9 that is 0.3% or 4 us, with intervals that overlap; the six changes fewer in each layer are 2.3 us of it by their price, and the rest is not told apart.

### The weights' loads beside the `y12` loads: e3

The changed kernel with the three loads of the mixing weights behind the norm's root again.

> The changed kernel with the mixing weights' three loads issued behind the root of the gate's norm, as before, still into their own home. Theory 3 (these loads share the DMA engines with the y_rows loads of layer 0): the y_rows loads of layer 0 fall from 15.3 us to 9 to 13 us, the total by 2 to 6 us minus what the gate waits for the weights (0 to 9 us, since the weights come 20 us later). Rival (the y_rows loads wait for something else): loads of layer 0 stay at 15 us and the total is equal or 5 to 9 us longer.

Measured: 1262.5 us. Down to combination in layer 0 fell from 12.2 to 9.9 us, and the `y12` loads took 13.2 us and not 15.3. In e7 and e12, also without the early loads, they took 14.3 and 14.5; in e10, with them, 13.8. So sharing the engines costs 1 or 2 us, not the bulk of the delay. The gate then waits for the masks again (from the first product behind the last combining one to its end 45.6 us and not 34.2). Theory 3's mechanism is there, the price of avoiding it is higher.

### Both put right: e17, e18

> The kernel of e16_combine_sorted with the first pair by token products in the sorted order of e15_tiles_sorted, list 1 ahead of them, list 2 behind them, list 3 behind pair 0's gate/up (the order of e5_lists_ahead). Theory (the first pair's change fails by its order, not by its idea): membership table to first gate/up 9.5 to 11 us, first gate/up to last down 239 to 243 us as with the gather, total 1206 to 1212 us, at or below the 1212.65 of e16_combine_sorted. Rival (what follows the token products costs more than the gather whatever their order): 1214 us or more.

> The kernel of e16_combine_sorted with the first pair as in e15_tiles_sorted (token products sorted, the lists as the change put them, two of them among pair 0's gate/up products). If the lists among pair 0's products and the clock there cost about 5 us a layer, as first gate/up to last down of e15_tiles_sorted says (244.1 and 250.0 us against 240 and 242): 1217 to 1227 us, 5 to 14 us above e16_combine_sorted. Rival (the place of the lists does nothing, e17_all and this one agree within 2 us).

Measured: 1222.8 and 1226.9 us, both 10 us or more behind e16 with its gather. Token products in the sorted order reach the first gate/up sooner than the gather (9.6 and 11.0 us against 13.1 and 11.4), and lose it again between first gate/up and last down (244 to 247 us against 240 to 242). In the marks of e17 against e16 that is 4 us in all. Another 6 us are not the first pair's: in layer 1 down to combination is 17.7 and 18.5 us against 11.9, but the last `y12` load had landed at 1150.5 in e17 and the additions were done at 1152.2. What held the combination until 1158.5 were the ten idle products of e9:

```profile
1147.53 11.18 PE L1489 MATMUL ps<-scr_sb,const_sb 128*128 128x512 f32 x20 [4.78 <-issue]
```

They start behind 4.8 us in which TensorE waits for nothing that the profile shows (1.4 us in e16) and take 11.2 us, part of it at the low clock, where e16's take 8.9. e18 has the same. Without that, e17 would be some 4 us behind e16 by these marks, an estimate and no run. The lists' place makes 4 us between the medians of the two kernels and 2.5 us by the ratios, with intervals that overlap: unclear.

Why the block behind the token products is longer, the timelines do tell. From pair 1 on, one pair's gate/up products start 13.3 to 13.4 us after the other's in every kernel here, for the first four pairs. What differs is the time from pair 0's first gate/up product to pair 1's: 16.4 or 18.0 us in the kernels that gather (before, e1, e6 to e9, e11 to e13, e16), and 19.5 to 23.9 us in those with token products. With two lists among pair 0's products it is 19.6 us where the clock is 1.00 throughout them (layer 0 of e10 and e14) and 23.4 to 23.9 with a long low stretch (after, e2, layer 1 of e15). Moving the lists out of them (e5, e17) leaves 20.2 to 22.2: list 3 then stands between pair 0 and pair 1, and in layer 0 of e17 TensorE waits 2.7 us for VectorE there. From pair 1's first product to the last down step all kernels are within 221.0 to 224.4 us in layer 0 and 223.8 to 226.6 in layer 1.

## Why the prediction was wrong

**Region 1, routing to first pair (forecast +5.7; it cost +26 in the marks of the changed kernel, +19.5 us alone).** Two steps failed. The one with the larger price is what the sum put at nothing: the low clock, kept as rival C with "+5 in a layer". The other is "32 and 16 of them, with the latter taken at 0.15, give 6.6 us". The 0.133 and 0.17 of [rows 5] come from a stretch with one change of rows. In the new stretch the row count changes fifteen times, and each change costs 0.19 us at the full clock: 8.5 us. The Trainium skill (TensorEngine Tiling (Array Packing), Key Properties) says that changing the tiling mode drains TensorE. By that rule the term would have been dearer, e14 and e15 agree with it, and I had not weighed it. The waits around it were right (1.2 and 2.0 us, table to gate/up 13.6 in layer 1 with 11.8 forecast, the rest 1.9 of it by the passes), and so was the exponential: it ran right behind its table load (229.37 + 1.28, then 230.66), and from the last routing product to the first table it is 0.6 us more than before, where 1.0 was forecast. The two lists were priced at 2.5 us; pair 0's gate/up passes went from 7.1 to 10.3 us where the clock held (e10 and e14, layer 0), 3.2 more, and to 15.8 and 14.6 where it did not.

**Rival C** had the right place and a fraction of the size. It took the low clock as a surcharge on 48 passes, +5 a layer. In layer 0 the clock stayed at 1.2 GHz for 27 us (237.2 to 264.5), through lists and pair 0 too. By the marks it cost 6.0 us ahead of the first gate/up product of layer 0 (19.6 against layer 1's 13.6) and 5.6 and 4.3 us in pair 0 (15.8 and 14.6 against 10.3): some 16 us, beside 3.8 for the changes of rows and 1.4 for the lists beyond their price. Why it falls for so long in some executions stays open. My reason against it, that dense passes stand ahead of the gap, was tried (e4, e10) and does not carry: with four and three more such products the clock still fell, later and for 3.4 to 6.8 us at a time, as it did in e3 with nothing put in.

**That a delay here shifts the block** was right, and e13 shows it one to one. What I did not do was to let the low clock count through it.

**Region 2 (forecast -12.3 and -12.1, measured -6.2 and -9.3).** The zero scatter, the early issue (8.4 us behind the scatter of pair 14, forecast 8) and the last pair without a wait on its loads came as said. The step that failed is "the 8.9 that they took (497.07 to 505.96)" with 1.0 on top: 15.3 us in layer 0, 1 to 2 of it the mixing weights' loads (e3), and 13.0 in layer 1. The reading was also short: by their landings the six loads took 9.8 us before. In [rows 6] they ran against little else; now they start beside the last slots. Rival B had the late transfers in the wrong place: it is not the last pair's slots that are late but the loads. That the stream is what slows them is not shown: in layer 0 it moved 0.55 MB in the first 4 us beside 0.43 MB of these loads, and 0.06 MB in the next 4. Their last 4 us move next to nothing (last section).

**Region 3 (forecast 21.9 in layer 1, 24.4 in layer 0; measured 23.7 and 29.6 to the gate's second tile).** The passes were sized right: with the clock at 1.00 throughout the stretch takes 20.9 us (e8). What failed is the clock again, put at nothing in layer 1 and at 5 to 6 us in layer 0: it was low for 5.8 and 18.5 us of the stretch, which cost 2.8 and 8.7 us. That is rival D in one of two layers, at a price of 8.7 and not 16, since the later tiles ran at the full clock. For both layers that makes +20.5 us where +13.5 was taken, against -15.5 for the wait where -24.4 was taken. The choice failed with the sizes: moving the addition to TensorE costs more behind the wait than the wait gives back (e7, above).

**Region 4 (forecast -8.8)** had the right mechanism and was more than paid: layer 0's gate needs 32.3 us from its second tile and not 44.9, -12.6. By itself the weights' home gives 7.3 us (e11). But it is no gain of its own beside the last pair's change, which takes away the same wait (e7).

**The end (forecast -1.2)** can't be told apart: from the gate's last product to the end 20.8 us against 21.0.

**The sum.** By the timed kernels: weights' home -7.3, last pair -0.6, what is left of the change without the first pair -2.5 (e1: -10.4 in all), first pair +19.5. That makes +9; the changed kernel has +14.5 by its own ratio. The 5 us between are not explained; the first pair costs 25 us on top of the rest and 19.5 alone. Of the 29 us between the forecast's -14.7 and this, 14 to 19 are the first pair's beyond its +5.7, and 10 the last pair's, forecast at -11 and worth -0.6. By the marks of the two profiled executions: region 1 +26.2, region 2 -15.5, region 3 +20.5, region 4 -12.1 (layer 1's +0.5 in it), the end -0.2, +0.6 between the layers, and -6.2 ahead of the first table, most of it the spread of attention. That is the 13.3 us between the spans.

## What to carry to other kernels

Before pricing a row of small products, count the changes of row count in it, not the passes alone: sort them so that equal shapes stand together, which took 10 us off this kernel (5.4 of them by the price of the changes) and cost nothing. Ahead of a stretch that is bound by a stream of transfers with a full buffer, every microsecond that delays the first frees is paid in full, so a shorter way with denser TensorE work can be slower than a longer one with an idle engine. And a shorter wait is worth only what the work behind it doesn't give back: time the two apart, since the addition that was moved from VectorE to TensorE made the last pair's change worth 0 and not 11 us.

## What the runs showed of the hardware

- A change between passes on 128 rows and on 32 rows costs 0.19 us at the full clock. Equal passes of 128 columns start 0.112 us apart at 2.4 GHz (0.213 at 1.2 GHz); each change lengthens two of these distances, to 0.20 to 0.21 (0.35 to 0.38).
- The granted clock stayed at 1.2 GHz for 27 us while TensorE shows busy in all but 2 us of it, on passes of 128, 4 and 512 columns, and for 18 us in the combination. The same first pair had 1.00 through its token products in e3. 512-column products in an idle stretch held it in e8 (both layers) and did not in e10 (layer 1).
- The six `y12` loads take 9.4 to 10.1 us in the kernels where they wait for the last pair (before, e2, e11), and 11.0 to 17.1 us where they are issued ahead of its down products; the last of that moves little data. In layer 1 of the changed kernel they go out from 1167.0 to 1169.6, the transfer engines are busy at first, then nearly idle, and the first combining product still waits until 1180.3 (windows as above, and the transfer queues from 1176 to 1180):

```profile
1168.00:1172.00 4.00, 3.58 (x10) 1.06 (x12) 0.00 (x0) 0.37 (x1) 2.16 (x5) 0.63 0.94 348
1172.00:1176.00 4.00, 1.77 (x8) 0.38 (x4) 0.75 (x1) 2.06 (x3) 0.00 (x0) 0.93 0.79 269
1176.00:1180.00 4.00, 0.00 (x0) 0.00 (x0) 0.00 (x0) 0.12 (x1) 0.00 (x0) 0.50 0.07 30
...
q0 software_dynamic: 37, 0.12, 7.4%
```

At 1176 to 1180 the engines are 0.07 busy with 30 GB/s, and all 37 packets are of the queue that brings the `y12` loads: nothing else is in their way, and a share of 0.07 of 16 engines is about one engine's time. Two loads land after 1179 (1179.3 and 1180.0). Why so few packets are left over for so long was not tried; it is some 4 us in each layer that the kernel before did not have: there, in layer 0, the engines are 0.83 busy from 503 to 506 and the last load lands at 506.9.
